# Retention in pairs of heads, four score banks in turn and two buffers, and another order of the first transfers

## The reference

```python
def retention_block(state, q, k, v):
    log_g = jnp.log1p(-jnp.exp2(-5.0 - jnp.arange(RET_HEADS, dtype=jnp.float32)))
    diff = n[:, None] - n[None, :]
    decay = jnp.where(diff >= 0.0, jnp.exp(jnp.maximum(diff, 0.0)[None] * log_g[:, None, None]), 0.0)
    scores = jnp.einsum('bnhd,bmhd->bhnm', qf, kf) * decay[None]
    o = jnp.einsum('bhnm,bmhv->bnhv', scores, vf)
    ...
    new_state = jnp.exp(t * log_g)[None, :, None, None] * state + jnp.einsum('bmhd,bmhv->bhdv', k_dec, vf)
```

## Time and profile before

| | us |
|---|---|
| median of 3 runs (2697.0 to 2700.9) | 2698.48 |
| the profiled execution | 2698.97 |
| its span, first to last instruction | 2696.9 |
| TensorE busy | 2446.3 (91%) |
| VectorE busy | 1266.8 (47%) |
| ScalarE busy | 891.6 (33%) |
| GpSimd busy | 869.1 (32%) |

### The profile page before, as it was taken

One profiled execution on the slowest core, in us unless ns is written; L12 is line 12 of the kernel. 1 busy time (PEld: TensorE's weight loads), 2 busy tenths in 40 slices (PEclk: granted clock), 3 DMA queues, 4 the chain that ended last, 5 costly groups with the idle time before them and its releaser, 6 DMA issues.

```text
span 2696.9 us, 46442 instructions
## 1 busy us (share of the span) xinstructions
PE 2446.3 (91%) x17558; PEld 2274.6 (84%) x17558; DVE 1266.8 (47%) x2072; ACT 891.6 (33%) x1308; POOL 869.1 (32%) x366
## 2 busy tenths in 40 slices
PE   1999999699888899999979999978988898999996
PEld 1999999599455899999979999978964577999996
DVE  6332388754364242327252325884724615333462
ACT  2443322324043434432244432223322234434321
POOL 0334334244000433334423333442420023333443
PEclk9999999899799999999989999999989998999998
DMA  6222277223000122226312224851220011222461
GB/s 211 71 86 86 91 250 265 67 80 121 1 32 1 47 78 86 86 88 236 128 48 86 86 81 167 278 178 52 85 72 32 1 32 48 87 84 89 157 215 54
DMA packets 71514, 272.52 MB, mean 101 GB/s; under 512 B 8640, under 2 KB 10048, under 8 KB 70528
## 3 DMA queue, kind: packets, MB, share of 16 engines
q1 hardware_dynamic: 71424, 271.35, 29.6%
HBM read 267.87 MB, written 3.45 MB: 101 GB/s over the span
## 4 chain that ended last, share of the span: by engine, by line
PE 53%; issue 28%; DVE 7%; POOL 7%; ACT 2%; DVEq 0%; POOLq 0%; DMA 0%; ACTq 0%; SPq 0%
PE ps L489 14%; PE ps L490 14%; PE ps L493 14%; POOL w_lo L425 6%; PE ps L697 2%; PE ps L661 2%; PE ps L786 2%; PE ps L742 2%; DVE wide_v L1248 1%; DVE wide_v L1161 1%; PE ps L738 1%; PE ps L499 1%; DVE wide_rinv L1192 1%; PE ps L740 1%; DVE wide_rinv L1412 1%
## 5 line engine op out<-in xcount | busy, mean ns | idle before, releaser
L425 POOL TENSOR_TENSOR w_lo<-raw,w_hi 128x1024 fp32r<-128x1024 f32 (+1 forms) x304 | 789.9, 2599 | 1696.9 <-ACT w_hi L858 1414.6
L489 PE MATMUL ps<-h_hi,w_hi 128*128 128x274 f32 (+1 forms) x3488 | 953.5, 291 | 18.9 <-DVE h_lo L1203 18.4
L490 PE MATMUL ps<-h_lo,w_hi 128*128 128x274 f32 (+1 forms) x3488 | 953.7, 291 | 0.0
L493 PE MATMUL ps<-h_hi,w_lo 128*128 128x274 f32 (+1 forms) x3488 | 727.0, 290 | 0.0
L489 PEld LDWEIGHTS ps<-h_hi,w_hi 128*128 128x128 f32 x3488 | 665.2, 191 | 24.7 <-DVE h_lo L1203 23.7
L490 PEld LDWEIGHTS ps<-h_lo,w_hi 128*128 128x128 f32 x3488 | 660.1, 189 | 0.4
L858 ACT CAST w_hi<-raw 128x1024 fp32r<-128x1024 f32 (+1 forms) x244 | 277.0, 1135 | 845.9 <-PE ps L493 633.5
L493 PEld LDWEIGHTS ps<-h_hi,w_lo 128*128 128x128 f32 x3488 | 552.2, 189 | 0.0
L489 PE MATMUL ps<-u_hi,w_hi 128*128 128x272 f32 x1408 | 383.3, 291 | 12.8 <-POOL w_lo L425 12.7
L490 PE MATMUL ps<-u_lo,w_hi 128*128 128x272 f32 x1408 | 380.4, 288 | 0.0
L1161 DVE CUSTOM_DVE_ANT_0 wide_v<-ada_w,ps 128x1024 bf16<-128x1024 f32 x288 | 332.0, 1217 | 50.6 <-DMA ada_w<-in_ada 22.2
(11 more groups left out here) (205 smaller groups left out, 2389.6 us busy)
## 6 DMA issues: line engine op xcount, KB each, us to landing
raw<-in_w_up SPq DMA_DIRECT2D x176, 512.0 KB, 3.5
ada_w<-in_ada SPq DMA_DIRECT2D x160, 512.0 KB, 4.5
raw<-in_w_dn SPq DMA_DIRECT2D x64, 704.0 KB, 5.0
raw<-in_w_mix SPq DMA_DIRECT2D x64, 512.0 KB, 3.5
decay<-in_decay SPq DMA_DIRECT2D x2, 2048.0 KB, 8.1
x<-in_x SPq DMA_DIRECT2D x1, 2176.0 KB, 12.8
rope_tab<-in_rope SPq DMA_DIRECT2D x2, 1088.0 KB, 5.0
out_y<-x SPq DMA_DIRECT2D x1, 2176.0 KB, 6.6
```

Of the source, the lines that this page charges most:

```text
L425: pool.tensor_tensor(w_lo[:, slot, 0:width], raw[:, slot, 0:width], w_hi[:, slot, 0:width].bitcast(F32), ALU.subtract).then_inc(lo_done.se ...
L489: pe.matmul(ps[:, bank + t, 0:half], wh, hi[:, n], start=start, stop=False)
L490: pe.matmul(ps[:, bank + t, 0:half], wh, lo[:, n], start=False, stop=False)
L493: last = pe.matmul(ps[:, bank + t, 0:half], wl, hi[:, n], start=False, stop=stop)
```

## The change

**Retention.** The loop goes over 16 steps n instead of eight heads: pair i = n // 4, block b = n % 4. A step's scores are two matmuls, one for each head of the pair, into banks 2(b % 2) and 2(b % 2) + 1. VectorE multiplies both heads in one instruction, into one of two buffers. Scores of step n + 2 are issued ahead of the values of step n. `k_tok` stands on VectorE between blocks 0 and 1 of a pair, the state updates behind block 3. `ret_st0` lies where `ret_st` was, `ret_st1` over the rotary tables.

```diff
-                def ret_scores(h):
-                    rows = slice(64 * (h % 2), 64 * (h % 2) + 64)
-                    for b in range(4):
-                        if h:
-                            pe.wait_ge(rs_mul.sem, rs_mul.at(l, 4 * (h - 1) + b + 1))
-                        pe.matmul(ps[:, b, 0:512 - b * P], ret_k[rows, h // 2, b * P:(b + 1) * P],
-                                  ret_q[rows, h // 2, b * P:512], start=True, stop=True).then_inc(rs_mm.sem, 1)
+                def ret_scores(n):
+                    i, b = n // 4, n % 4
+                    if n >= 2:
+                        pe.wait_ge(rs_mul.sem, rs_mul.at(l, n - 1))
+                    for hh in range(2):
+                        rows = slice(64 * hh, 64 * hh + 64)
+                        last = pe.matmul(ps[:, 2 * (b % 2) + hh, 0:512 - b * P], ret_k[rows, i, b * P:(b + 1) * P],
+                                         ret_q[rows, i, b * P:512], start=True, stop=True)
+                    last.then_inc(rs_mm.sem, 1)
+
+                def ret_values(n):
...
+                    pe.wait_ge(rs_mul.sem, rs_mul.at(l, n + 1))
+                    w = 512 - b * P
+                    for hh in range(2):
+                        rows = slice(64 * hh, 64 * hh + 64)
+                        last = pe.matmul(ps[rows, 6 + i % 2, b * P:512], v_tok[:, b, i * P + 64 * hh:i * P + 64 * hh + 64],
+                                         ret_st[i % 2][:, hh, ST_AT[b]:ST_AT[b] + w], start=b == 0, stop=b == 3)
...
                 ret_scores(0)
...
+                ret_scores(1)
+                for n in range(16):
+                    if n < 14:
+                        ret_scores(n + 2)
+                    if n % 4 == 0:
+                        state(n // 4)
+                    if n % 4 == 2:
+                        state_mm(n // 4)
+                    ret_values(n)
```

and on VectorE:

```diff
+                def decayed(n):
+                    i, b = n // 4, n % 4
+                    if b == 0 and i >= 2:
+                        dve.wait_ge(ro_mm.sem, ro_mm.at(l, i - 1))
+                    dve.wait_ge(rs_mm.sem, rs_mm.at(l, n + 1))
+                    w = 512 - b * P
+                    v_.tensor_tensor(ret_st[i % 2][:, :, ST_AT[b]:ST_AT[b] + w], ps[:, 2 * (b % 2):2 * (b % 2) + 2, 0:w],
+                                     decay[:, 2 * i:2 * i + 2, 0:w], ALU.mult).then_inc(rs_mul.sem, 1)
```

```diff
+            sp.dma_start(ada_b[:, :], a["ada_b"]).then_inc(const_first.sem, 16)
+            sp.dma_start(g_pre[:, :], a["g_pre"]).then_inc(const_first.sem, 16)
+            for t in range(ADA_RING, 12):
+                sp.wait_ge(ada_done.sem, 2 * (t - ADA_RING + 1))
+                load_ada(t, t % ADA_RING)
             sp.dma_start(x[:, :, :], a["x"]).then_inc(x_in.sem, 16)
+            for t in range(12, 16):
+                sp.wait_ge(ada_done.sem, 2 * (t - ADA_RING + 1))
+                load_ada(t, t % ADA_RING)
...
             dve.wait_ge(c_act.sem, 1)
-            dve.wait_ge(const_in.sem, 16 * N_CONST)
+            dve.wait_ge(const_first.sem, 32)
...
             dve.wait_ge(x_in.sem, 16)
+            dve.wait_ge(const_in.sem, 16 * N_CONST)
```

More of the change, by code:

```diff
@@ L102, in overlay @@
                             inner, more = overlay(item)
+                            room = "room_" + next(iter(inner))
+                            scope.enter_context(nc.sbuf_tensor(room, [P, more // 4], F32))
                             made.update(inner)
@@ L162, in streaming_trunk @@
             [("decay", [P, HEADS, 512], F32), ("q_cross", [P, 4, 2, NS], F32), ("ret_ss", [NS, HEADS, NS], F32),
-             ("k_toks", [NS, 4, P], F32), ("k_tok", [P, 4, P], F32), ("ret_st", [P, 4, 512], F32)],
+             ("k_toks", [NS, 4, P], F32), ("k_tok", [P, 4, P], F32), ("ret_st0", [P, 2, TRI], F32)],
             [("ret_root", [P, 4, T], F32)],
@@ L193, in streaming_trunk @@
             um[n] for n in ("kpe_swap", "q_pe_swap", "rope_tab", "v_tok", "state_in", "zq"))
-        qn_hi, qn_lo, state_p, k_tok, ret_st = um["qn_hi"], um["qn_lo"], um["state_p"], hm["k_tok"], hm["ret_st"]
+        qn_hi, qn_lo, state_p, k_tok = um["qn_hi"], um["qn_lo"], um["state_p"], hm["k_tok"]
+        ret_st = [hm["ret_st0"], um["ret_st1"]]
         ret_root, q_cross, ret_ss, k_toks = hm["ret_root"], hm["q_cross"], hm["ret_ss"], hm["k_toks"]
@@ L1372, in mixer @@
                     .then_inc(ss_mul.sem, 1)
[L1373 to L1398, removed]
@@ new lines, in mixer @@
+                for i in range(4):
+                    decayed(4 * i)
+                    dve.wait_ge(kt_mm.sem, kt_mm.at(l, 2 + i))
+                    if i:
+                        dve.wait_ge(st_mm.sem, st_mm.at(l, i))
+                    v_.tensor_tensor(k_tok[:, :, :].rearrange("p b (h d) -> p b h d", h=2),
+                                     ps[:, 4, :].rearrange("p (b h d) -> p b h d", b=4, h=2),
+                                     k_decay[:, i, :, :].unsqueeze(3).to_broadcast([P, 4, 2, RDK]), ALU.mult)\
+                        .then_inc(kt_ev.sem, 1)
+                    decayed(4 * i + 1)
+                    decayed(4 * i + 2)
+                    decayed(4 * i + 3)
+                    dve.wait_ge(st_mm.sem, st_mm.at(l, i + 1))
+                    for hh in range(2):
+                        r = slice(64 * hh, 64 * hh + 64)
+                        v_.tensor_copy(state_p[r, i, :], ps[r, 5, hh * VD:(hh + 1) * VD]).then_inc(st_ev.sem, 1)
+                        v_.scalar_tensor_tensor(out=state_in[r, i, :], in0=state_in[r, i, :],
+                                                scalar=state_decay[r, i:i + 1],
+                                                in1=ps[r, 5, P + hh * VD:P + (hh + 1) * VD],
+                                                op0=ALU.mult, op1=ALU.add).then_inc(st_ev.sem, 1)
```

36 lines of the change are left out of this document (22 added, 14 removed).

## The result

The changed kernel took 2652.59 us (median of four runs, 2650.41 to 2653.54), the kernel before 2697.74 on the same chip (2694.67 to 2700.9, four runs): a ratio of 0.9831 with a 95% interval of 0.9814 to 0.9848, 45 us less. The forecast was 2650, the range 2643 to 2664. The profiled execution took 2653.0, with a span of 2650.9.

The account below looks back on a forecast made before the run. TensorE was taken to bound the kernel, on 53% of the chain that ended last. From 2698.97 us, two retention cores save 41.7 and the start 7.0, giving 2650.3, forecast as 2650; range 2643 to 2664.

Parts of the forecast that it names:

- What bounds: Whole kernel: TensorE is on 53% of the chain; an edit pays only where it stands still or streams more than needed.
- Side by side: Retention core: both heads of a pair stream at once, scores and values each at one head's 2.1 us a pair.
- The entry into a group: Retention core: each TensorE entry into a group of another shape costs about 0.25 us.
- VectorE's holes: Retention core: TensorE waits for VectorE twice a pair, 0.6 us behind `k_tok` and 0.35 us behind the state instructions.
- The clock: Retention core: the rise from 1.2 GHz comes after 5 to 10 us, which costs 3 us against the 37.2.
- The start: Program start: with constants and `x` moved behind tiles, VectorE starts at 11.3, 7.0 us earlier, and the moved transfers stay hidden.
- The rest shifts along: Later work: all of it shifts along; where TensorE's clock falls in attention may differ by some 2 us.
- 1, values apart: Retention core: the heads' values don't stream together; a core of 45, total 2659; chance 0.15 together with "5, the buffers don't decouple".
- 2, clock stays low: Retention cores: clock low for 20 us of each, 2659, or throughout, 2689; chance 0.13, a third of it beyond 2665.
- 3, no overlap: Retention core: neither scores nor values overlap; 48 us at full clock, 54 with slow beginning, total 2677; chance 0.06.
- 4, slower through drains: Retention core: each change of shape drains TensorE; at 1.0 us a change the total is 2710; chance 0.03.
- 5, the buffers don't decouple: Retention core: VectorE's queue holds every block, 4 us a core more, total 2658; chance 0.15 together with "1, values apart".

Follow-up runs that it names:

- the start alone: The kernel before with only the new order of the first transfers, retention core and buffers as they were; 2690.65 us against 2692.75, ratio 0.9990.

## Why the prediction was right, point by point

**What bounds.** Right: the gain came from the stretch where TensorE stood still or filled half of the array. VectorE took over a part of it, 4.2 us of waits in a core of 37.6, as the prediction had it.

**Side by side.** Right for both. For the scores the nearest row was of the same form, and 512 columns for two heads took 1.06 to the next start. For the values the row showed only a short stream beside a long one, and the prediction took the lower bound, 2.1 us a pair, against 4.2. That was a guess between two bounds. The values' run on one half of the columns shows that it was the right end: 1.08 against 1.93.

**The entry into a group** was set at 0.25 and is smaller. The timeline of the kernel with VectorE's new order has no holes between groups behind the first 4 us of its core. From a group's start to the next one's, the scores of blocks 1, 2 and 3 take 0.84, 0.63 and 0.42 (block 0's 1.06 is in the changed kernel's timeline), 2.95 where 3.1 was forecast. The values take 1.01, 0.80, 0.59 and 0.37, 2.77 where it was 3.1. The slope is 0.21 for 128 columns of two passes, as forecast, and what is left is 0.21 and 0.16 an entry. The 0.25 was what two equations left over, from groups of twenty and of eight passes. The state matmuls' group of eight still takes 1.09 and so still has it. Why the groups of two heads have less no run shows.

**VectorE's holes.** Both places are right. The first was 0.64 for 0.6, the second 0.53 for 0.35. Streaming came to 7.9 a pair and not 8.3, so TensorE arrives earlier and waits longer. That ate part of what the smaller entry gave, and a pair is 9.1 instead of 9.3.

**The clock.** Direction right, size too cautious: 3.7 us at the lower level and not 5 to 10. The core is 37.6 and not 40.5, the term that was mis-sized most: 47.4 saved and not 41.7. At full clock it is 35.8 (four times 7.9, four holes of 0.64 and three of 0.53) where 37.2 was forecast, and the low beginning costs 1.9 and not 3. So the miss is about half the pairs' and half the clock's. (37.2 and 3 are 40.2; where the other 0.3 of 40.5 comes from the prediction doesn't say.) The reason that it gave, the whole array in use, was argued from one trace. The runs fit it for the rows: 2.7 to 6.1 us wherever the scores stand on both halves, 10.8 and more wherever they don't. It did not see that 20 of the 45 us at the lower level in the old cores were later falls. Against what the old core takes in other executions (55.7 once in four) it would be less: the four unchanged cores in the two traces are 60.0 in the mean, which gives 44.7.

**The start.** VectorE at 10.87 for 11.3, right, and the `raw` load did no harm: issued at 44.81, it had landed before VectorE had its columns ready, which ScalarE waited for last (to 52.22). The step that failed is `x`. The prediction had its landing between 6.6 and 12.8 us, took the tile behind it as in time, and kept the late tile for a case of 0.03. It took 10.8 us, tile 12 was 2.7 late, and the term was 4.9 and not 7.0 (4.9 to 6.4 in the five traces with `x` whole behind tile 11). With `x` in four pieces it is 6.9. Where a range of landings has its need in the middle, the lateness at the longer end belongs in the sum.

**The rest shifts along.** Only nearly: 6.3 us of the 52.3 went in the stretches outside, which is within what one execution differs from the next. The two misses of the sum, 5.7 more saved and 2.1 less, and this one took each other away, so that 2650 came so close to 2652.6 is in part luck.

**The rivals.** 1, values apart: refuted, and its price was too high, a core of 41.1 and not 45, because their length fills the holes. 2, clock stays low: refuted for the changed kernel in six cores (3.2 to 4.5 us), but seen in the run with scores on one half. 3, no overlap: refuted by both runs on one half. Its 48 us at full clock doesn't follow from the prediction's own terms, which give 4 x (8.3 + 4.2) = 50. 4, slower through drains: refuted. A pair has eleven groups where it had seven, and an entry into scores or values costs at most 0.21. TensorEngine Tiling of the Trainium skill, Key Properties, has the rule that a change of tiling mode drains the engine. The trace can't tell a drain from whatever else an entry holds. All together is 0.16 to 0.21 us, so four more entries cost a pair less than 0.9 us (an estimate), against 4.2 us of streaming that it saves. 5, the buffers don't decouple: refuted, though what holds the two blocks is just what it named, VectorE's queue.

## What to carry to other kernels

Two fp32 matmuls whose contraction fills half of the rows, or whose outputs fill half of the columns, belong next to each other on different halves: each pair cost what one had cost. With the rows' halves filled the clock also rose sooner. Once TensorE's work per block shrinks, what stands ahead of its supplier in that engine's queue sets the time. Moving two small steps behind the multiply that TensorE waits for gave 9.5 us more in the cores and 11.7 in the time, at no cost. A second buffer was worth 2.7 us a core with pairs; look first at how many holes it closes.

## What the runs showed of the hardware that was not expected

- Two full streams of 512 fp32 columns on two halves of the output columns take no longer than one: 1.08 us for four passes, against 1.93 on one half.
- How long the 1.2 GHz level held on from a core's first matmul followed the placing of the scores, with TensorE busy nearly all the time: 2.7 to 6.1 us with both halves of the rows in use (eighteen cores), 10.8 to 13.4 head by head (six), 30.2 and 11.2 with scores on one half. That is what the runs show; no run here tells what in the placing does it.
- One and the same core took 55.7 and 61.6 us, for the clock alone, and runs of the kernel before lay between 2683.78 and 2698.75 on one chip. A difference of 5 us needs many runs: the start gain of 5.4 us seen in the trace could not be shown in the time with 12 runs of the start alone.
- A transfer of 2176 KB took 8.8 to 10.8 us between tiles of 512 KB, where `out_y` alone took 6.6, and held up the tile behind it by 0.6 to 2.7; as four pieces of 544 KB (7.0 each) it held up nothing.
